# Feed-forward of a streaming encoder step on one core: split weight operands kept in DRAM by the first block and loaded by the others, with the first steps and block borders reordered

## Chip, cores and metric

The kernel runs on one core of one Trainium2 chip. The metric is the device time of one execution in microseconds. Three runs of the kernel before gave 2531.25, 2531.59 and 2532.89 us; their median is 2531.59 us.

## The reference, cut to what matters

All arrays are fp32: 2048 prompt positions and 64 sample positions, model width 1024, one layer. The change lies in the second half of the layer, the convolutional feed-forward, which takes some 1540 of the 2529 us:

```python
def causal_dwconv(u, prev, w):            # width 3, along positions
    up = jnp.concatenate([prev.astype(u.dtype), u], axis=1)
    y = up[:, 0:L] * w[0]
    for t in range(1, width):
        y = y + up[:, t:t + L] * w[t]
    return y, up[:, L:]

def conv_ffn(xn, prev, w_up, conv_w, w_down):     # w_up 1024 x 5632, w_down 2816 x 1024
    u = xn @ w_up
    uc, new = causal_dwconv(u, prev, conv_w)
    a, g = jnp.split(uc, 2, axis=-1)
    return (jax.nn.silu(g) * a) @ w_down, new

    x = x + mixer(rmsnorm(x, norm1))              # first half: gated short convolution and GLA heads
    x = x + conv_ffn(rmsnorm(x, norm2))
return rmsnorm(x, final_norm)
```

## The kernel before

**Blocks.** The positions go through the kernel in three blocks, NB = 3: 768, 768 and 512 + 64 (with a gap of 2 columns between prompt and sample). First all three blocks go through the mixer, then all three through the feed-forward. A block has 6, 6 and 5 tiles of 128 rows (the last of block 2 has 64, and TensorE works on it in another way).

**fp32 from fp32r.** Every product is made of three matmuls on fp32r operands: each operand is split into a high part (ACT's Copy to fp32r) and a low part (operand minus high part, in fp32r), and high x high, low x high and high x low are added (`product`, L1282 to L1284, the lines of the three matmuls).

**Steps.** A feed-forward block has NF = 22 steps; step f makes 128 columns of a and 128 of g from x, and adds their share of the output. `ffn_step` is written once for each engine (SP, POOL, ACT, PE, DVE), and the engines run through the same steps in their own order with semaphores between them. g in the code counts steps over the blocks, g = b * NF + f. Steps 2 to 19 are a hardware loop; steps 0, 1, 20, 21 are written out.

**Seven products.** The up projection of a step is a 2 x 2 block matrix product (columns a and g by two halves of the block's positions, `HALF` = 384, 384, 290, and two halves of the 1024 input features) that is done with seven products instead of eight (a Strassen-Winograd scheme). Its weight operands are three raw quarters (`A_RAW`) and four sums of quarters (`A_SUM`); its x operands are likewise three pieces and four sums, which were written to the DRAM tensor `x_ops` in the mixer stage (`combine` makes the sums S1 to S4 on DVE). Operand i of the weights belongs to product i. A product is 4 x 3 matmuls over 128x128 weights. Its results go to PSUM and are put together with the helpers r_1 (ACT), r_2 and r_3 (DVE); product 2 waits for r_1, 3 for r_2, 5 for r_3, because of the banks.

**Weights of a step.** SP loads the four quarters with two DMAs (`load_up`, L539, to `wu_raw`, one buffer), two steps ahead. DVE makes four sums (`sum_up`, L1639 to L1645, to `wu_sum`). ACT makes seven high parts (`high_up`, L899), POOL seven low parts in two instructions each (`low_up`, L795). The results, `wq_hi` and `wq_lo`, have one buffer per operand: operand i of the next step can be made once product i of this step is done. This is done in every step of every block, 66 times, with the same 22 weight tiles in each block. The w_down tile (128 x 1024) comes by one DMA and is split by ACT (L1237) and POOL (L820).

**Down products.** 12 (block 2: 10) per step, one for each tile and half of 512 columns; each is 3 matmuls (the 64-row tile 2). They are spread over the following two steps by `head_shares` and `tail_shares` (how many after each of the seven products), and use four PSUM banks, which come free when DVE has added the result to `resid` (`add_down`, L1880). `finish_up` on ACT and DVE is the chain from u to the hidden values: taps (L1897), silu (L937), the product with a (L1906); `high_hidden` and `low_hidden` split the hidden values.

**Block borders.** In the last step of a block SP loads the next block's seven x operands (`load_x_op`, L543), each after the product that used its place; in this and the next step ACT splits them (`high_x`) and DVE or POOL makes the low part (`low_x`: DVE 0, 1, 3, 5 in L1630, POOL 2, 4, 6 in L803). In steps 0 and 1 of a block the last block's output is normalised (`final_rstd` on ACT, with a change of the activation table; `final_scale` on DVE, L1608), stored, and the residual tiles of the new block are loaded (`load_resid`); DVE waits for them (`resid_ready`).

**The order.** No scheduler: every engine's order is the order of the text. SP issues all DMAs, on one queue, and where a DMA has to wait for a semaphore, all behind it wait. The lines that say when a step's weights are loaded and when a step's sums are made:

```python
sp.wait_ge(wu_summed, 4 * (g + 2))          # SP, at the end of its step
sp.wait_ge(wu_lo, NP * (g + 1) + 6)
load_up(b, f + 2 ...)
sum_up(g + 1, 0); sum_up(g + 1, 1)          # DVE, between r_2 and r_3
```

## Time and profile before

| | busy us | share of the span | instructions |
|---|---|---|---|
| TensorE matmul (PE) | 2359.5 | 93% | 13090 |
| TensorE weight load (PEld) | 2141.1 | 85% | 13090 |
| VectorE (DVE) | 1802.6 | 71% | 2588 |
| GpSimd (POOL) | 1516.2 | 60% | 1489 |
| ScalarE (ACT) | 1073.9 | 42% | 2059 |

The profiled execution took 2530.73 us, with a span of 2529.0 us from the first to the last recorded instruction. Its mean granted TensorE clock was 0.978 of full. It moved 231 MB, 92 GB/s on average.

The page's slices show the stages (each digit is the busy share of 1/40 of the span, 63 us, in tenths; the feed-forward begins in the 16th):

```profile
PE   7999999999999995999999988999999978888896
DVE  2045670355624566889888897888888879999998
POOL 3132423222343237887788795888888877777773
PEclk9999999999999998999999998999999989999998
```

A busy share counts matmuls with their modelled ends, so a PE that is busy throughout has no gap, but says nothing of how fast one matmul is. Shares are averages over stages with different limits.

### The profile page before, as it was taken

To read this page: it belongs to the slowest core of one execution; us is meant where nothing else is said; L and a number is where in the kernel's file an instruction comes from. 1 tells how busy PE (TensorE), PEld (TensorE's weight loads), DVE (VectorE), ACT (ScalarE), POOL (GpSimd) and SP (SyncE) were. 2 spreads that over 40 slices of the span, in tenths; PEclk is the share of its full clock that TensorE was granted. 3 is DMA by queue.
4 is the path that set the end of the run, shared out by engine and by line. 5 is a ranking of instruction groups with operands and counts; after the bars stand their busy time and mean duration, and the time that the engine had idled before them with its cause. 6 is when DMAs were issued, how large, how long until landed. Compare 5 with 4: busy or idle time off the path is not lost. (4 is left out here: it accounts for less than half of the span.)

```text
span 2529.0 us, 39169 instructions
## 1 busy us (share of the span) xinstructions
PE 2359.5 (93%) x13090; PEld 2141.1 (85%) x13090; DVE 1802.6 (71%) x2588; ACT 1073.9 (42%) x2059; POOL 1516.2 (60%) x1489
## 2 busy tenths in 40 slices
PE   7999999999999995999999988999999978888896
PEld 6899878898798974999999977999999967787785
DVE  2045670355624566889888897888888879999998
ACT  4233353333543335444444455444444464444443
POOL 3132423222343237887788795888888877777773
PEclk9999999999999998999999998999999989999998
DMA  5121334112361146222221244222122432222221
GB/s 158 51 59 43 125 136 143 43 43 101 115 193 51 60 142 230 68 67 75 75 67 57 75 137 150 75 75 75 50 75 75 141 120 74 74 77 75 77 74 65
DMA packets 244718, 231.43 MB, mean 92 GB/s; under 512 B 8060, under 2 KB 216273, under 8 KB 244625
## 3 DMA queue, kind: packets, MB, share of 16 engines
q1 hardware_dynamic: 244625, 230.18, 28.9%
q8 instruction: 60, 0.98, 0.2%
q14 instruction: 33, 0.27, 0.0%
HBM read 197.32 MB, written 32.83 MB: 91 GB/s over the span
## 5 line engine op out<-in xcount | busy, mean ns | idle before, releaser
L1282 PE MATMUL ps<-xo,wq_hi 128*128 128x384 f32 (+1 forms) x1848 | 607.4, 329 | 92.7 <-DVE r L1960 42.3
L795 POOL TENSOR_TENSOR wq_lo<-wu_sum,wq_hi 128x256 fp32r<-128x256 f32 x528 | 478.4, 929 | 213.4 <-ACT wq_hi L899 207.4
L1283 PE MATMUL ps<-xo,wq_lo 128*128 128x384 f32 (+1 forms) x1848 | 603.7, 327 | 0.0
L1284 PE MATMUL ps<-xo,wq_hi 128*128 128x384 f32 (+1 forms) x1848 | 603.3, 326 | 0.0
L458 POOL TENSOR_TENSOR w_lo<-raw,w_hi 128x512 fp32r<-128x512 f32 x192 | 251.0, 1333 | 576.6 <-ACT w_hi L451 576.6
L1880 DVE TENSOR_TENSOR resid<-resid,ps 128x512 f32<-128x512 f32 (+1 forms) x748 | 487.1, 678 | 17.7 <-PE ps L1284 6.2
L1282 PEld LDWEIGHTS ps<-xo,wq_hi 128*128 128x128 f32 x1848 | 355.4, 192 | 127.7 <-issue 73.3
L795 POOL TENSOR_TENSOR wq_lo<-wu_raw,wq_hi 128x256 fp32r<-128x256 f32 x396 | 406.0, 1045 | 35.6 <-ACT wq_hi L899 35.5
L1283 PEld LDWEIGHTS ps<-xo,wq_lo 128*128 128x128 f32 x1848 | 355.7, 192 | 19.1
L1897 DVE SCALAR_TENSOR_TENSOR up_y<-up_u,params,up_y 128x768 f32<-128x768 f32 (+1 forms) x264 | 321.9, 1219 | 49.7 <-ACT up_y L929 26.0
L1284 PEld LDWEIGHTS ps<-xo,wq_hi 128*128 128x128 f32 x1848 | 356.0, 193 | 0.0
L1282 PE MATMUL ps<-xt_hi,w_hi 128*128 128x384 f32 (+4 forms) x960 | 317.0, 330 | 6.8 <-DVE xt_lo L1622 3.8
L1283 PE MATMUL ps<-xt_hi,w_lo 128*128 128x384 f32 (+4 forms) x960 | 310.5, 323 | 0.0
L1284 PE MATMUL ps<-xt_lo,w_hi 128*128 128x384 f32 (+4 forms) x960 | 310.3, 323 | 0.0
L899 ACT ACTIVATE wq_hi<-wu_sum 128x512 fp32r<-128x512 f32 x264 | 163.4, 627 | 318.2 <-DVE wu_sum L1641 204.3
L1282 PE MATMUL ps<-wd_hi,hid_hi 128*128 128x512 f32 x704 | 279.8, 397 | 14.5 <-DVE resid L1880 13.9
L1284 PE MATMUL ps<-wd_lo,hid_hi 128*128 128x512 f32 x704 | 279.9, 398 | 0.0
L1283 PE MATMUL ps<-wd_hi,hid_lo 128*128 128x512 f32 x704 | 277.8, 395 | 0.0
L1282 PEld LDWEIGHTS ps<-xt_hi,w_hi 128*128 128x128 f32 x960 | 182.4, 190 | 19.0 <-issue 8.9
L1283 PEld LDWEIGHTS ps<-xt_hi,w_lo 128*128 128x128 f32 x960 | 182.6, 190 | 5.4 <-issue 0.5
L1284 PEld LDWEIGHTS ps<-xt_lo,w_hi 128*128 128x128 f32 x960 | 182.3, 190 | 5.1
L820 POOL TENSOR_TENSOR wd_lo<-wd_raw,wd_hi 128x512 fp32r<-128x512 f32 x132 | 181.9, 1398 | 2.7 <-ACT wd_hi L1237 2.7
(197 smaller groups left out, 3818.2 us busy)
## 6 DMA issues: line engine op xcount, KB each, us to landing
wu_raw<-in_w_up_dram SPq DMA_DIRECT2D x132, 512.0 KB, 5.0
raw<-in_w_in_dram SPq DMA_DIRECT2D x72, 512.0 KB, 3.8
wd_raw<-in_w_down_dram SPq DMA_DIRECT2D x66, 512.0 KB, 5.7
x_in<-in_x_prompt_dram SPq DMA_DIRECT2D x32, 512.0 KB, 4.4
raw<-in_w_out_dram SPq DMA_DIRECT2D x24, 512.0 KB, 3.3
xo_raw<-x_ops SPq DMA_DIRECT2D x14, 768.0 KB, 5.7
x_mid<-resid SPq DMA_DIRECT2D x16, 512.0 KB, 2.8
resid<-x_mid SPq DMA_DIRECT2D x16, 512.0 KB, 6.2
```

The costliest lines, as they stand in the source:

```text
L458: last = pool.tensor_tensor(w_lo[:, s, r], raw[:, s, r], w_hi[:, s, r].bitcast(F32), ALU.subtract)
L795: last = pool.tensor_tensor(wq_lo[:, i, r], src[:, r], wq_hi[:, i, r].bitcast(F32), ALU.subtract)
L820: last = pool.tensor_tensor(wd_lo[:, par, r], wd_raw[:, r], wd_hi[:, par, r].bitcast(F32), ALU.subtract)
L899: act.activation(wq_hi[:, i, :], wu_source(i), ACT.Copy).then_inc(wu_hi, 1)
L1282: pe.matmul(out, lh, rh, start=(first and n == 0), stop=False, skip_group_check=skip)
L1283: pe.matmul(out, ll, rh, start=False, stop=False, skip_group_check=skip)
L1284: last = pe.matmul(out, lh, rl, start=False, stop=end, skip_group_check=skip)
L1880: last = dve.tensor_tensor(resid[0:m, t, s], resid[0:m, t, s], ps[0:m, bank, :], ALU.add)
L1897: dve.scalar_tensor_tensor(y, up_u[:, m, tap:tap + w], params[:, FFN_TAP + tap, bass.ds(m * NF + f, 1)], y, ALU.mult, ALU.add).then_inc(su ...
```

## The change

- `wq_hi` and `wq_lo` become one tensor `wq` [128, 7, 2, 512], in which the high and low part of an operand lie side by side (`WQ_AT` is the place of operand i).
- A new DRAM tensor `w_ops` holds, for each of the 22 steps, the seven finished operands (high and low, 128 x 4 KB, 0.52 MB each). `KEPT` says which are kept (all seven), `SPLIT` which are still made in each block (all in block 0, none in blocks 1 and 2).
- Block 0: after the low part of operand i SP stores it (`store_op`). ACT's `high_up` waits until the store of the same operand of the step before has read it (`op_stored`).
- Blocks 1 and 2: `high_up` and `low_up` return at once and `sum_up` isn't called. SP loads operand i of the next step in place once product i of this step is done (`load_op`); PE waits for `op_loaded`.
- First step of all: the split of operand 1 moves up; r_1 is copied by ACT before the other x operands (`keep_first_product`); x operands 4, 5 and 6 are split inside step 0; the second half of the last `combine` moves behind r_2; `load_up(0, 1)` and the loads of x operands 5 and 6 move ahead of the stores of the sums, the first w_down tile behind them. The stores of step 0's operands 0 to 5 stand behind that.
- Block borders: `low_x(6)` moves from POOL to DVE. Of the final norms in step 1, tiles 4 and 5 move up on ACT and DVE, with one activation table change fewer, and SP issues their stores and residual loads between the operand loads (`results`).
- Last step of all: no down products of the step before in it; all 10 come behind it.

The diff, cut to its core (declarations, renamed arguments, blank and most unchanged lines are left out):

```diff
@@ -77,6 +77,11 @@
 S1, S2, S3, S4 = 0, 1, 2, 3
 A_RAW = {0: 0, 2: 1, 5: 3}
 A_SUM = {1: S2, 3: S3, 4: S1, 6: S4}
+WQ_AT = [0, 1, 4, 5, 2, 3, 6]
+KEPT = (0, 1, 2, 3, 4, 5, 6)
+SPLIT = [tuple(range(NP))] + 2 * [tuple(i for i in range(NP) if i not in KEPT)]
 X_SUM = {4: 0, 1: 1, 3: 2, 5: 3}
...
@@ -136,11 +141,15 @@
...
+    if b == NB - 1 and isinstance(f, int) and f == NF - 2:
+        return shares([0] * NP, 0)
...
+    if b == NB - 1 and isinstance(f, int) and f == NF - 2:
+        return shares([2 * TILES[b]], 0)
...
@@ -490,6 +503,15 @@
...
+        def after(b, f):
+            return (b + 1, 0) if is_last(f) else (b, f + 1)
+        def splits(b, f, i):
+            steps = NP * f if b == 0 else NP * NF + len(SPLIT[b]) * ((b - 1) * NF + f)
+            return steps + sum(n <= i for n in SPLIT[b])
...
@@ -536,12 +558,36 @@
...
+            def kept(f, i):
+                return w_ops[bass.ds(f, 1), 1 + KEPT.index(i)].rearrange("o p s c -> p (o s) c")
+            def store_op(f, i):
+                sp.wait_ge(wu_lo, splits(0, f, i))
+                sp.dma_start(kept(f, i), wq[:, WQ_AT[i]].bitcast(F32)).then_inc(op_stored[KEPT.index(i)], 16)
+            def load_op(b, f, i):
+                sp.wait_ge(up_done, NP * (b * NF + f - 1) + i + 1)
+                sp.wait_ge(op_stored[KEPT.index(i)], 16 * NF)
+                sp.dma_start(wq[:, WQ_AT[i]].bitcast(F32), kept(f, i)).then_inc(op_loaded[KEPT.index(i)], 16)
...
@@ -653,50 +699,79 @@
...
+                if b == NB - 1:
+                    sp.wait_ge(wu_lo, splits(0, 0, 5))
+                    load_up(0, 1)
                 sp.wait_ge(x_sums, sums_before(b + 1))
+                if b == NB - 1:
+                    sp.wait_ge(ops_stored, 16 * 3 * NB)
+                    for i in range(5, NP):
+                        load_x_op(0, i)
                 for i, n in X_SUM.items():
...
+                if b == NB - 1:
+                    second[b].wait(sp, "turned", 2 * nt)
+                    sp.wait_ge(sums_stored, 16 * 4 * NB)
+                    load_down(0)
...
+                if b == 0 and edge == 0:
+                    for i in KEPT:
+                        if i < 6:
+                            store_op(f, i)
                     for t in range(TILES[0]):
                         load_resid(0, t)
-                wait(sp, wd_low, g)
-                sp.dma_start(wd_raw[:, :], w_down[0, bass.ds(f * P, P), :]).then_inc(wd_loaded, 16)
...
+                else:
+                    wait(sp, wd_low, g)
+                    load_down(f)
+                if b == 0:
+                    store_op(f, 6)
+                nb, nf = after(b, f)
+                then = after(nb, nf)
+                for i in range(NP):
+                    if edge == NF - 1 and b + 1 < NB:
                         sp.wait_ge(up_done, NP * g + i + 1)
                         load_x_op(b + 1, i)
...
+                    if more and i in KEPT:
+                        if nb:
+                            load_op(nb, nf, i)
+                        elif i < 6:
+                            store_op(nf, i)
...
+                    if edge == 1 and b and i in (1, 3):
+                        results(b, range(i + 1, min(i + 3, TILES[b - 1])))
+                if load and not nb and SPLIT[then[0]]:
+                    sp.wait_ge(wu_lo, splits(nb, nf, 5))
+                    load_up(*then)
+                if edge == 0 and b:
+                    results(b, range(2))
...
@@ -788,11 +863,13 @@
...
-            def low_up(g, i):
-                pool.wait_ge(wu_hi, NP * g + i + 1)
+            def low_up(b, f, i):
+                if i not in SPLIT[b]:
+                    return
+                pool.wait_ge(wu_hi, splits(b, f, i))
                 src = wu_source(i)
                 for r in (slice(0, 256), slice(256, 512)):
-                    last = pool.tensor_tensor(wq_lo[:, i, r], src[:, r], wq_hi[:, i, r].bitcast(F32), ALU.subtract)
+                    last = pool.tensor_tensor(wq[:, WQ_AT[i], 1, r], src[:, r], wq[:, WQ_AT[i], 0, r].bitcast(F32), ALU.subtract)
                 last.then_inc(wu_lo, 1)
...
@@ -823,33 +900,26 @@
...
+            low_up(0, 0, 0)
+            low_up(0, 0, 1)
             low_x(0, 2)
...
-            low_x(0, 6)
+            for i in range(2, NP - 1):
+                low_up(0, 0, i)
...
                 if first_f:
                     low_x(b, 4)
                 for i in range(NP - 1):
                     if more:
-                        low_up(g + 1, i)
-                    if i == 4:
+                        low_up(*after(b, f), i)
+                    if i == (5 if first_f and b == 0 else 4):
                         low_down(g, par)
-                        if first_f:
-                            low_x(b, 6)
                 if is_last(f) and b + 1 < NB:
                     low_x(b + 1, 2)
...
@@ -895,8 +965,27 @@
...
-            def high_up(g, i):
-                act.activation(wq_hi[:, i, :], wu_source(i), ACT.Copy).then_inc(wu_hi, 1)
+            def high_up(b, f, i):
+                if i not in SPLIT[b]:
+                    return
+                g = b * NF + f
+                if i in A_RAW:
+                    act.wait_ge(wu_loaded[A_RAW[i] // 2], 16 * (g + 1))
+                    if b == 0 and i == 5:
+                        act.wait_ge(wu_summed, 4 * g + 4)
+                else:
+                    act.wait_ge(wu_summed, 4 * g + A_SUM[i] + 1)
+                if b == 0 and i in KEPT:
+                    wait(act, op_stored[KEPT.index(i)], 16 * g)
+                act.activation(wq[:, WQ_AT[i], 0], wu_source(i), ACT.Copy).then_inc(wu_hi, 1)
+            def keep_first_product(b, g, par):
+                h = HALF[b]
+                act.wait_ge(up_done, NP * g + 1)
+                wait(act, c21_read, g)
+                act.activation(r_1[:, 0:h], ps[:, 3 * par, 0:h], ACT.Copy).then_inc(r1_read, 1)
...
@@ -1168,75 +1264,69 @@
...
+                            high_up(0, 0, 0)
+                            high_up(0, 0, 1)
                         if j == 2:
                             high_x(0, 1)
...
-                            high_up(0, 1)
-                        if j == 4:
                             high_x(0, 2)
-                        if j == 5:
-                            high_up(0, 2)
+                        if j == nt:
+                            mix.wait(act, "out_done", 8 * nt)
+                            high_up(0, 0, 2)
+                            keep_first_product(0, 0, 0)
...
+            high_up(0, 0, 3)
+            high_x(0, 3)
+            high_up(0, 0, 4)
+            high_up(0, 0, 5)
...
-                high_up(g, 6)
+                if not first_of_all:
+                    keep_first_product(b, g, par)
+                high_up(b, f, 6)
                 if prev:
                     high_hidden(*prev, 1 - par)
-                if edge == 0 and b:
+                if edge == 0:
                     high_x(b, 4)
...
-                    act.preload_act_table(ACT.Silu)
...
+                    act.wait_ge(up_done, NP * g + 1)
+                    high_up(nb, nf, 0)
                     act.wait_ge(up_done, NP * g + 2)
-                    act.wait_ge(wu_summed, 4 * (g + 1) + S2 + 1)
-                    high_up(g + 1, 1)
+                    high_up(nb, nf, 1)
                 act.wait_ge(up_done, NP * g + 3)
                 wait(act, taps_a, 2 * g)
                 act.activation(up_u[:, 0, 2:2 + h], ps[:, 3 * par, 0:h], ACT.Copy).then_inc(c11_read, 1)
                 earlier_rows(b, 0, f)
-                if edge == 0 and b:
+                if edge == 0:
                     high_x(b, 5)
                 if more:
-                    high_up(g + 1, 2)
+                    high_up(nb, nf, 2)
                     act.wait_ge(up_done, NP * g + 4)
-                    act.wait_ge(wu_summed, 4 * (g + 1) + S3 + 1)
-                    high_up(g + 1, 3)
+                    high_up(nb, nf, 3)
                     act.wait_ge(up_done, NP * g + 5)
-                    high_up(g + 1, 4)
...
+                    high_up(nb, nf, 4)
+                if not first_of_all:
+                    high_down(b, f, par)
+                if edge == 0:
                     high_x(b, 6)
+                if edge == 1 and b:
+                    for t in range(4, TILES[b - 1]):
+                        final_rstd(b - 1, t)
+                    act.preload_act_table(ACT.Silu)
...
@@ -1247,13 +1337,15 @@
...
+                    high_up(nb, nf, 5)
+                if first_of_all:
+                    high_down(b, f, par)
...
-                if edge in (0, 1) and b:
+                if edge == 0 and b:
                     act.preload_act_table_set("natural_log_exp_and_others")
-                    for t in range(2) if edge == 0 else range(4, TILES[b - 1]):
+                    for t in range(2):
                         final_rstd(b - 1, t)
...
@@ -1542,7 +1634,10 @@
...
-                    pe.wait_ge(wu_lo, NP * g + i + 1)
+                    if i in SPLIT[b]:
+                        pe.wait_ge(wu_lo, splits(b, f, i))
+                    else:
+                        pe.wait_ge(op_loaded[KEPT.index(i)], 16 * (g - NF + 1))
...
@@ -1858,15 +1955,17 @@
...
-                    if b == NB - 1:
-                        for c0, w in PIECES[b].get(j - 2, []):
-                            n2.wait(dve, "hi", 2 * (j - 2))
-                            done = combine(c0, w)
+                    if b == NB - 1 and j == nt:
+                        n2.wait(dve, "scaled", nt)
+                        sum_up(0, 1)
+                        n2.wait(dve, "hi", 2 * 3)
+                        done = combine(b, *PIECES[b][3][0], done)
...
@@ -1921,9 +2020,11 @@
...
-            sum_up(0, 1)
             low_x(0, 3)
-            low_x(0, 5)
+            def last_combine():
+                second[NB - 1].wait(dve, "hi", 2 * TILES[NB - 1])
+                combine(NB - 1, *PIECES[NB - 1][5][0], sums_before(NB - 1) + 4)
...
@@ -1948,18 +2049,20 @@
...
                 dve.tensor_tensor(r_2[:, 0:h], ps[:, 1, 0:h], r_1[:, 0:h], ALU.add).then_inc(r2_read, 1)
+                if edge == 0 and b == 0:
+                    last_combine()
...
                 adds(1)
-                if more:
+                if b == 0 and not is_last(f):
                     sum_up(g + 1, 0)
                     sum_up(g + 1, 1)
                 adds(2)
                 dve.wait_ge(up_done, NP * g + 4)
                 dve.tensor_tensor(r_3[:, 0:h], ps[:, 1, 0:h], r_1[:, 0:h], ALU.add).then_inc(r3_read, 1)
...
-                if edge == 0 and b:
+                if edge == 0:
                     low_x(b, 5)
...
@@ -1967,6 +2070,11 @@
...
                 adds(4)
+                if edge == 0:
+                    low_x(b, 6)
+                if edge == 1 and b:
+                    for t in range(4, TILES[b - 1]):
+                        final_scale(b - 1, t)
...
```

## Rows read from the trace of the kernel before

**Rows 1.** The windows view, core 0: stretch, busy us, instructions, clock, DMA share, GB/s.

```profile
1080.00:1440.00 360.00, 360.00 (x1895) 336.76 (x1894) 322.10 (x412) 152.15 (x254) 286.63 (x286) 1.00 0.22 67
1600.00:1980.00 380.00, 380.00 (x2000) 355.45 (x2000) 330.74 (x435) 164.01 (x302) 311.39 (x298) 1.00 0.23 70
2077.81:2480.22 402.41, 358.27 (x2129) 321.52 (x2128) 368.26 (x534) 180.09 (x446) 310.92 (x361) 0.97 0.26 78
2480.22:2497.32 17.10, 16.77 (x108) 15.38 (x106) 15.63 (x25) 5.89 (x17) 9.26 (x10) 1.00 0.09 32
...
957.62:1025.29 67.67, 38.14 (x200) 35.47 (x200) 44.71 (x43) 30.54 (x48) 56.15 (x54) 0.82 0.60 206
1481.56:1580.94 99.38, 78.29 (x362) 71.19 (x361) 78.18 (x90) 52.72 (x90) 73.24 (x68) 0.88 0.36 119
2014.39:2077.81 63.42, 45.49 (x239) 40.22 (x237) 50.49 (x63) 36.76 (x70) 48.68 (x50) 0.87 0.38 126
...
970.00:994.00 24.00, 6.30 (x23) 6.33 (x24) 8.89 (x10) 8.91 (x10) 17.32 (x20) 0.53 1.00 347
1464.00:1470.00 6.00, 6.00 (x33) 5.51 (x32) 5.97 (x9) 2.78 (x5) 5.44 (x6) 1.00 0.98 374
```

**Rows 2.** The timeline of PE, block 2: first matmul of a product, down product, product.

```profile
2166.36 0.29 PE L1282 MATMUL ps<-xo,wq_hi 128*128 128x290 f32 x1
...
2167.97 0.39 PE L1282 MATMUL ps<-wd_hi,hid_hi 128*128 128x512 f32 x1
...
2169.34 0.29 PE L1282 MATMUL ps<-xo,wq_hi 128*128 128x290 f32 x1
```

**Rows 3.** Groups by line and form, DVE, 2100 to 2480: busy us, mean ns.

```profile
L1897 DVE SCALAR_TENSOR_TENSOR up_y<-up_u,params,up_y 128x578 f32<-128x578 f32 x73 | 92.3, 1264 | 18.6 <-ACT up_y L929 13.3 <-DVE up_y L1897 3.8
...
L1639 DVE TENSOR_TENSOR wu_sum<-wu_raw 128x512 f32<-128x512 f32 x18 | 20.4, 1133 | 0.0
L1641 DVE TENSOR_TENSOR wu_sum<-wu_sum,wu_raw 128x512 f32<-128x512 f32 x18 | 20.0, 1113 | 0.6
...
L1643 DVE TENSOR_TENSOR wu_sum<-wu_raw 128x512 f32<-128x512 f32 x18 | 13.3, 740 | 0.0
```

**Rows 4.** Who waited for whom, 2100 to 2480: us in total, times, longest.

```profile
PE ps L1282 <- DVE r L1960: 28.5, 16, 1.9
```

**Rows 5.** Groups by form, DVE, 2500 to 2503, where POOL does nothing.

```profile
L1897 DVE SCALAR_TENSOR_TENSOR up_y<-up_u,params,up_y 128x578 f32<-128x578 f32 x2 | 1.6, 822 | 0.1
```

**Rows 6.** The timeline of PE at start and border 0/1; in brackets the idle time before.

```profile
987.70 0.66 PE L1282 MATMUL ps<-xo,wq_hi 128*128 128x384 f32 x1 [21.35 <-ACT r L1203]
...
996.74 0.41 PE L1282 MATMUL ps<-xo,wq_hi 128*128 128x384 f32 x1 [0.27 <-DVE r L1960]
...
1518.09 0.66 PE L1282 MATMUL ps<-xo,wq_hi 128*128 128x384 f32 x1 [5.43 <-issue]
...
1542.09 0.56 PE L1282 MATMUL ps<-xo,wq_hi 128*128 128x384 f32 x1 [4.79 <-DVE r L1960]
...
1564.85 0.79 PE L1282 MATMUL ps<-wd_hi,hid_hi 128*128 128x512 f32 x1 [5.01 <-DVE resid L1880]
```

**Rows 7.** The timeline of SP, POOL and DVE, single lines.

```profile
972.33 3.75 SPq L658 DMA_DIRECT2D x_ops<-tst  x4
...
1512.69 5.29 POOL L803 TENSOR_TENSOR xo<-xo_raw,xo 128x384 fp32r<-128x384 f32 x4
...
1703.42 0.80 DVE L1639 TENSOR_TENSOR wu_sum<-wu_raw 128x512 f32<-128x512 f32 x1
...
1718.37 1.00 SPq L539 DMA_DIRECT2D wu_raw<-in_w_up_dram  x2
```

**Rows 8.** The page's DMA issues: KB each, median us from issue to landing.

```profile
wu_raw<-in_w_up_dram SPq DMA_DIRECT2D x132, 512.0 KB, 5.0
...
x_mid<-resid SPq DMA_DIRECT2D x16, 512.0 KB, 2.8
```

120 lines of the change are left out of this document (49 added, 71 removed).

## The prediction, made before the changed kernel ran

> **What bounds the kernel now.** The windows view comes first, cut at the borders that PE's timeline shows. In the middle of block 0's feed-forward PE is busy 360.00 of 360 us at granted clock 1.00 [rows 1]; 1895 matmuls make 0.190 us each, so a step of 120 matmuls (7 products of 12, 12 down products of 3) takes 22.8 us. Block 1's middle is the same (2000 matmuls in 380.00 us). Nothing that ACT, DVE, POOL or SP is spared there shortens the step. In block 2 (steps 2 to 20) PE is busy 358 of 402 us at clock 0.97, and DVE 368 [rows 1]: 21.18 us a step. Its floor: a product of 12 matmuls of 290 columns takes 2167.97 - 2166.36 = 1.61 us, six down matmuls 2169.34 - 2167.97 = 1.37 us [rows 2], so 84 x 0.134 + 28 x 0.228 = 17.7 us. The waits view names who holds PE: product 5, behind DVE's r_3 (L1960), 1.8 us in 16 of 18 steps [rows 4]; after it the clock is at the lower of its two levels for some matmuls, which is how 1.8 us become 3.5. DVE is late because of the four sums of sum_up, which stand just ahead of r_3: 20.4 + 20.0 + twice 13.3 (L1643; L1645 has the same) = 67.0 us over 18 steps, 3.7 us a step [rows 3]. The last step of all is the experiment in the old kernel: no sums, POOL nearly empty, 17.10 us with PE busy 16.77 [rows 1].
>
> The other losses are the borders, three stretches that [rows 1] hold as well: start of block 0 (957.62 to 1025.29, PE busy 38.1 of 67.7), border 0/1 (1481.56 to 1580.94, 78.3 of 99.4), border 1/2 (2014.39 to 2077.81, 45.5 of 63.4). All three also run at clock 0.82 to 0.88.
>
> **Part 1: no split in blocks 1 and 2.** Gone: 44 x 7 high parts on ACT, 44 x 14 low halves on POOL, 44 x 4 sums on DVE. Block 1's middle: 0 us, since PE is full. Block 2: DVE is busy 368.26 / 19 = 19.4 us a step, less 3.7 is 15.7 us, at the pace it has beside POOL, plus 18.6 / 18 = 1.0 us of waits before the taps [rows 3]: 16.7 against PE's 17.7. PE takes over. But the margin of 1.0 us is thin, and in the last step, with POOL still busy in its first part, PE still lost 0.3 us. So how fast DVE is without POOL matters. The taps (128x578) take 1264 ns in the middle of block 2 [rows 3] and 822 ns where POOL does nothing [rows 5]; four a step give 1.8 us more margin. I take 17.9 us a step (floor plus 0.2), bounds 17.7 (floor) and 19.4 (only the 1.8 us of idle go, and smaller waits keep pulling the clock down). 19 steps: 402.4 - 340.1 = **-62 us** (-67 to -34).
>
> The Trainium skill ("SBUF — State Buffer", section "Who interferes with whom") has the rule behind those taps: a VectorE instruction with two SBUF inputs and a GpSimd instruction that reads SBUF need the same read interface, and the one that comes second waits. 822 against 1264 ns is as the rule says. By it all the contended time goes away and the step sits at 17.7 to 17.9; without it DVE would keep 16.7 us of work, and I would take 18.4, a sum 10 us worse.
>
> **Part 2: what replaces it, transfers.** A step now loads 7 x 0.524 MB of operands and 0.524 MB of w_down: 4.19 MB, in block 2 in 17.9 us, 234 GB/s, where 78 is moved now [rows 1]. The trace has stretches with the queues full: 347 GB/s over 24 us, with stores among them, 374 over 6 us [rows 1]. PE is 6.00 of 6 us busy in the latter with 33 matmuls, 0.18 each, so full queues do not slow it. Each operand is asked for when PE has finished that product of the step before and is wanted a whole step less one product later, some 16 us, for a landing of 5.0 us [rows 8]. Hidden; cost 0, and if the rate fell under 234 GB/s it would show at once. SP's load of w_down now stands behind the load of operand 6, which waits for the step's last product; ACT wants it four products later, at least 10 us, and a load of this size lands in 5. Hidden.
>
> **Part 3: block 0 pays.** Seven stores of 0.524 MB a step: 5.24 MB in 22.8 us, 230 GB/s. The new wait, ACT's high part of operand i on the store of the previous step's, has a whole step of slack in the middle. The load of step f+2's weights now has one more store in front of it, 1.4 us at 374 GB/s: issued at 1718.37 and landed 5.0 us later at 1723.4 now, at about 1725 then; its first DVE reader comes at 1703.42 + 22.8 = 1726.2 [rows 7, 8]. Hidden by 1 us, and DVE has more slack after it. Cost 0, bounds 0 and +0.6 x 20 = +12 us.
>
> **Part 4: border 0/1.** Three steps of 120 matmuls at 0.190 are 68.4 us; 99.4 is taken. The stalls: product 6 of step 0 waits 5.43 us for low_x(6), which POOL ends at 1512.69 + 5.29 [rows 6, 7]; it stands behind seven low parts that go, and moves to DVE, which no longer has its sums. Product 5 of step 1 waits 4.79 us for r_3, behind two final scales and the four sums. In step 2 a down product waits 5.01 us for DVE, which stands at the wait for the residual tiles 4 and 5 [rows 6]; their final scales and stores move up by some 5 us. I let 8 us stay (the taps chain of step 0, final scales): **-23** (-12 to -29). What is late next is the wait for gated and low_x(3), 2 to 3 us.
>
> **Part 5: border 1/2.** Floor: 168 x 0.134 + 69 x 0.228 = 38.2 us; 63.4 is taken. DVE is busy 50.5 us there, less two steps of sums 43.1. So DVE, not PE, is the next bound: I take 45, **-18** (-8 to -23).
>
> **Part 6: start of block 0.** Now PE idles 21.35 us before product 2, since ACT copies r_1 only after all x operands [rows 6]. The copy moves up behind high_up(2), to about 964. Walking the new order by hand at today's durations (low_x on POOL 5.3 us [rows 7]), product 2 can start at 967, product 3 at 971, product 4 at 979 (POOL's low_x(4)). But look at what product 5 waits for. ACT's order in step 0 is high_x(4), high_up of step 1's operands 0 and 1, copy c11, high_x(5). Those high_up wait for the stores of step 0's operands 0 and 1. SP issues these stores only behind load_down(0), and that stands behind the landing of the four sums (2.4 MB), which are issued at 972.33 now [rows 7], and in the new order after the last combine, which moves behind low_x(3) and r_2 (about 977), and behind x operands 5 and 6 (128 x 1536 fp32 each, 1.6 MB): 4 MB at 347 to 374 GB/s and about 2 us to land is 989, then 0.5 + 0.5 MB and landing (2.8 us for such a store [rows 8]): 993. All of ACT stands till then: the c11 copy, high_x(5), high_x(6). Product 5 starts about 998.5 (996.74 now [rows 6]), product 6 about 1002. So the 21 us that were idle before product 2 are idle before product 5. Then step 1: between 989 and the landing of step 2's weights SP moves 11.5 MB (w_down, 13 stores, 6 residual tiles, the weights): 31 us at 370, so about 1019 instead of 1012, and DVE's sums hold r_3 again. **+6 us** (-10 if the stores get through early, +14).
>
> **Part 7: the end.** Four down products move from the last step behind it. DVE is back to back there and has the same additions: 0 (±1).
>
> Sum: -62 - 23 - 18 + 6 = -97. The profiled execution took 2530.7 (span 2529.0 and 1.7 around it): 2433.4; the median lies 0.9 above it: **2434 us**.
>
> **Rivals.** (A) DVE keeps block 2: the chain finish_up, adds, r_2, r_3 is serial, and 19.4 us a step remain, with less at the borders (-17, -12): -34 - 29 + 6 = -57, 2475 us. For it: DVE is still busy 15.7 of 17.7. Against it: the last step. (B) The start gives time back: if SP's stores get through 10 us earlier than reckoned, or ACT's wait is met, product 5 starts near 985 and the start is 12 us shorter, not 6 longer: 2416. For it: everything but that one wait is ready. Against it: SP issues in order. (C) The other side: the transfers become the bound. The feed-forward moves 22 x 5.24 + 44 x 4.19 = 300 MB, with the borders some 325, in the 1540 us from 957 to 2497; at under 211 GB/s sustained it is longer than before. At 200 it is 325 / 0.200 - 1540 = 85 us longer, 2616. For it: no stretch in the trace keeps up such a rate for more than some 30 us. Against it: 347 over 24 us with writes among it. (D) Block 0's stores don't hide: 1.5 us a step over 20 steps, for example by the weights' landing past DVE's need: 2464.
>
> **Chances.** Forecast 0.62 (own range 2420 to 2450), A 0.12, B 0.12, C 0.04, D 0.10. Range 2412 to 2474: it takes in B and D, and ends at A; outside lie C and the far ends of A. About 0.2% (5 us) can be told from no change: faster 0.95, same 0.01, slower 0.04.
>
> **What would show it.** Block 2's steps at 17.7 to 18.1 us and clock 1.00, taps near 0.82 us there (A if 19.4); blocks 0 and 1 unchanged at 22.8 us a step (D if block 0 is longer); DMA near 230 GB/s through the feed-forward; the wait of product 6 at the borders gone; at the start ACT idle for some 15 us ahead of a wq high part, released by SP's store, and PE's long idle before product 5. The prediction is wrong if any step of blocks 1 or 2 waits for an operand's load, or if the start is shorter than before.

## The result, and the profile after

The changed kernel takes **2447.14 us** (median of 4 runs, 2444.29 to 2447.52), the kernel before 2532.24 us beside it: ratio 0.9662, 95% interval 0.9649 to 0.9675, 85.1 us less. The forecast was 2434 us in a range of 2412 to 2474. The profiled span went from 2529.0 to 2445.4 us. Cut at the first matmul of an up product (product 0 of the step named), the two traces and a third one (the reordering alone, experiment 1) give this table; the last two columns are differences, changed minus before:

| stretch, us | before | reordering alone | changed | forecast | measured |
|---|---|---|---|---|---|
| up to the first up product | 957.6 | 957.5 | 956.6 | 0 | -1.0 |
| start of block 0 (to step 2) | 67.7 | 62.5 | 82.3 | +6 | **+14.6** |
| rest of block 0 | 456.3 | 456.3 | 456.3 | 0 | 0 |
| border 0/1 (to step 3) | 99.4 | 88.5 | 80.9 | -23 | **-18.5** |
| rest of block 1 | 433.5 | 433.5 | 433.5 | 0 | 0 |
| border 1/2 (to step 2) | 63.4 | 58.0 | 46.4 | -18 | **-17.0** |
| block 2, steps 2 to 20 | 402.4 | 401.0 | 338.8 | -62 | **-63.6** |
| last step and end | 48.8 | 50.4 | 50.7 | 0 | **+2.0** |

The windows view of the changed kernel, columns as in [rows 1], which hold the matching stretches of before. In order: the middle of block 0, the middle of block 1, block 2 (steps 2 to 20), the start, border 0/1, border 1/2:

```profile
1080.00:1440.00 360.00, 360.00 (x1894) 336.64 (x1893) 322.53 (x411) 152.64 (x254) 284.80 (x282) 1.00 0.65 229
1600.00:1950.00 350.00, 350.00 (x1844) 327.46 (x1842) 236.72 (x339) 92.55 (x168) 69.95 (x62) 1.00 0.58 185
2055.89:2394.67 338.78, 336.99 (x2130) 314.12 (x2129) 271.35 (x465) 109.14 (x309) 80.58 (x95) 1.00 0.76 243
956.61:1038.87 82.26, 43.98 (x200) 40.50 (x200) 44.23 (x45) 30.25 (x48) 55.35 (x50) 0.75 0.81 290
1495.13:1575.99 80.86, 72.25 (x361) 64.84 (x360) 63.38 (x79) 38.76 (x67) 23.62 (x20) 0.98 0.73 268
2009.45:2055.89 46.44, 40.41 (x239) 36.77 (x237) 36.81 (x53) 27.78 (x57) 16.81 (x16) 0.96 0.76 267
```

In block 2 PE is busy 336.99 of 338.78 us at clock 1.00, where it was 358 of 402 at 0.97; DVE has 14.3 us of work a step (271.35 / 19) instead of 19.4. In the start the clock is at 0.75 and PE idle for 38 of 82 us, while the queues move 290 GB/s. By form, DVE's taps in block 2 (2100 to 2380, as [rows 3]):

```profile
L1996 DVE SCALAR_TENSOR_TENSOR up_y<-up_u,params,up_y 128x578 f32<-128x578 f32 x64 | 52.6, 822 | 14.9 <-ACT up_y L1018 10.2 <-DVE up_y L1996 3.3
```

The wait of product 5 for r_3 [rows 4] is gone from block 2: the longest wait of its steps 2 to 20 is 0.9 us, once, for an addition. The page's DMA issues (as [rows 8]):

```profile
wq<-w_ops SPq DMA_DIRECT2D x308, 512.0 KB, 3.8
w_ops<-wq SPq DMA_DIRECT2D x154, 512.0 KB, 2.7
```

The start in the timelines of ACT, SP, PE and DVE, in that order (the number in brackets is the idle time before, and who ended it):

```profile
968.59 1.47 ACT L994 ACTIVATE xo<-xo_raw 128x1536 fp32r<-128x1536 f32 x1
998.17 0.63 ACT L982 ACTIVATE wq<-wu_raw 128x512 fp32r<-128x512 f32 x1 [28.12 <-DMA w_ops<-wq]
...
978.41 6.35 SPq L712 DMA_DIRECT2D x_ops<-tst  x4
992.65 0.34 SPq L590 DMA_DIRECT2D wd_raw<-in_w_down_dram  x1
993.10 6.16 SPq L576 DMA_DIRECT2D w_ops<-wq  x6
...
1012.97 6.41 SPq L561 DMA_DIRECT2D wu_raw<-in_w_up_dram  x2
...
1003.69 0.66 PE L1374 MATMUL ps<-xo,wq 128*128 128x384 f32 x1 [17.97 <-issue]
...
1029.10 0.66 PE L1374 MATMUL ps<-xo,wq 128*128 128x384 f32 x1 [4.71 <-DVE r L2063]
...
1025.60 0.95 DVE L1736 TENSOR_TENSOR wu_sum<-wu_raw 128x512 f32<-128x512 f32 x1 [6.45 <-issue]
```

ACT stands 28.12 us before its first high part of step 1, until step 0's operand 0 is stored. The stores were issued at 993.10, behind w_down, which waited for the landing of the four sums. PE waits 17.97 us before product 5 (the view says "issue" because it sees no releaser; ACT's high part of x operand 5 ends at 1001.8 and DVE's low part at 1003.6). That is the forecast mechanism; but it is 5 us later, and a second one stands behind it: step 2's weights land at about 1025 (forecast 1019), and r_3 comes only behind DVE's sums of them.

### The profile page after: what moved, and what is told of

It reads as the page before. It is cut to its first block and busy times, and to the rows that moved or that the text cites. A ratio compares the mean times of both kernels' runs of the same rounds, so it can differ in the third digit from the quotient of the medians.

```text
span 2445.4 us, 39112 instructions
## 1 busy us (share of the span) xinstructions
PE 2332.6 (95%) x13090; PEld 2129.1 (87%) x13090; DVE 1583.6 (65%) x2415; ACT 906.9 (37%) x1747; POOL 919.7 (38%) x861
## 5 line engine op out<-in xcount | busy, mean ns | idle before, releaser
L1374 PE MATMUL ps<-xo,wq 128*128 128x384 f32 (+1 forms) x1848 | 600.0, 325 | 46.4 <-issue 18.6
L1375 PE MATMUL ps<-xo,wq 128*128 128x384 f32 (+1 forms) x1848 | 598.8, 324 | 0.0
L1376 PE MATMUL ps<-xo,wq 128*128 128x384 f32 (+1 forms) x1848 | 598.6, 324 | 0.0
L1374 PEld LDWEIGHTS ps<-xo,wq 128*128 128x128 f32 x1848 | 350.8, 190 | 68.2 <-issue 46.7
L1375 PEld LDWEIGHTS ps<-xo,wq 128*128 128x128 f32 x1848 | 351.3, 190 | 20.4
L1376 PEld LDWEIGHTS ps<-xo,wq 128*128 128x128 f32 x1848 | 351.3, 190 | 0.0
L1996 DVE SCALAR_TENSOR_TENSOR up_y<-up_u,params,up_y 128x768 f32<-128x768 f32 (+1 forms) x264 | 272.7, 1033 | 49.1 <-ACT up_y L1018 30.7
L897 POOL TENSOR_TENSOR wd_lo<-wd_raw,wd_hi 128x512 fp32r<-128x512 f32 x132 | 170.2, 1310 | 313.5 <-ACT wd_hi L1049 313.5
L1374 PE MATMUL ps<-wd_hi,hid_hi 128*128 128x512 f32 x704 | 277.5, 394 | 10.8 <-DVE resid L1979 10.4
L891 POOL TENSOR_TENSOR hid_lo<-up_y,hid_hi 128x384 fp32r<-128x384 f32 (+1 forms) x132 | 120.1, 931 | 254.4 <-ACT hid_hi L1042 254.4
L872 POOL TENSOR_TENSOR wq<-wu_sum,wq 128x256 fp32r<-128x256 f32 x176 | 161.9, 945 | 62.8 <-ACT wq L982 60.3
L1374 PE MATMUL ps<-w_hi,xt_hi 128*128 128x512 f32 (+1 forms) x408 | 163.7, 401 | 6.3 <-issue 2.9
```

The lines of the kernel that those rows point to most:

```text
L872: last = pool.tensor_tensor(wq[:, WQ_AT[i], 1, r], src[:, r], wq[:, WQ_AT[i], 0, r].bitcast(F32), ALU.subtract)
L891: last = pool.tensor_tensor(hid_lo[:, par, r], up_y[:, 0, r], hid_hi[:, par, r].bitcast(F32), ALU.subtract)
L897: last = pool.tensor_tensor(wd_lo[:, par, r], wd_raw[:, r], wd_hi[:, par, r].bitcast(F32), ALU.subtract)
L1374: pe.matmul(out, lh, rh, start=(first and n == 0), stop=False, skip_group_check=skip)
L1375: pe.matmul(out, ll, rh, start=False, stop=False, skip_group_check=skip)
L1376: last = pe.matmul(out, lh, rl, start=False, stop=end, skip_group_check=skip)
```

## Experiments

Times are medians; "the changed kernel" is 2447.1 us. Stretches are cut as in the table. Seven profiles with the changed kernel's start unaltered have 80.1 to 82.7 us there; among the kernels that leave the borders as they are, border 0/1 has 77.9 to 81.4 and border 1/2 45.1 to 47.8. So a single one of these stretches is known to some 2 us.

**1. The reordering without the keeping.**

```
-KEPT = (0, 1, 2, 3, 4, 5, 6)
+KEPT = ()
-                if b == 0 and not is_last(f):
+                if more:
                     sum_up(g + 1, 0)
```
(and the weights of every step loaded whole by `load_up`)

> The reorderings of the change without the keeping: every step of all three blocks loads and splits its weights as before the change (KEPT is empty, DVE's sums and POOL's low parts are back in blocks 1 and 2, no operand is stored or loaded). Theory (block 2's gain is the splitting's, the start's loss is the kept stores'): block 2's steps 2 to 20 stay near 402 us, start of block 0 near 60 to 66 us instead of 82.3 (67.7 before the change), since ACT is held by no store; border 0/1 some 8 us under the 99.4 of before, border 1/2 some 4 under its 63.4; in all 2532 - 4 - 8 - 4 = 2516 us (2505 to 2525). Rival 1 (the borders' gain is all the reordering's): 2532 - 4 - 18.5 - 17 = 2492. Rival 2 (the start's loss is the reordering's, not the stores'): the start stays near 80, and the time is 2532 + 12 - 12 = 2532.

Measured 2510.75 us, ratio to before 0.9919 (0.9902 to 0.9935), before at 2531.1 in this set: some 20 us of the 85 are the reordering's, some 65 the keeping's. The table's middle column splits them by place: the start gains 5.2 us by the reordering and loses 19.8 by the keeping; border 0/1 gains 10.8 and 7.7, border 1/2 5.4 and 11.6; block 2 1.4 and 62.2. Most of what the end lost (1.6 us) is the reordering's. Both rivals are out. Block 2 is as before the change, waits included (the second line is of the waits view: total, times, longest):

```profile
2056.28:2457.24 400.96, 355.60 (x2129) 318.77 (x2128) 367.26 (x533) 175.20 (x439) 310.83 (x363) 0.98 0.25 76
...
PE ps L1368 <- DVE r L2057: 34.2, 19, 1.9
```

**2 to 4. Which engine's work held block 2.** Idle work, whose result nothing reads, is put back into blocks 1 and 2 of the changed kernel (the waits around it are left out):

```
 low_up (POOL):  if i not in SPLIT[b]:
+    for r in (slice(0, 256), slice(256, 512)):
+        last = pool.tensor_tensor(wu_raw[:, 1 + 2 * (i % 2), r], wu_raw[:, 0, r], wu_raw[:, 2, r], ALU.subtract)
 ffn_step (DVE), where sum_up stood:
+if b:
+    for n in range(4):
+        dve.tensor_tensor(wu_sum[:, n, :], wu_raw[:, 0, :], wu_raw[:, 2, :], ALU.add)
```

> The changed kernel with POOL's work of blocks 1 and 2 put back as idle work: 14 subtractions of 128x256 a step on scratch that nothing reads, at the places of the low parts; no sums on DVE, no high parts on ACT, operands loaded as in the change. By the trace before the change DVE's 128x578 taps take 1264 ns beside POOL and 822 without it. Theory (the Trainium skill, "SBUF — State Buffer", section "Who interferes with whom": VectorE with two SBUF inputs waits for GpSimd's SBUF reads): the taps take 1.1 to 1.3 us again, DVE is busy some 16.4 us a step instead of 14.2, still under PE's 17.7, so block 2 runs at 17.9 to 18.5 us a step, 2449 to 2460 us in all. Rival 1 (it was the contention that made block 2 late): 19.5 or more a step, over 2478 us. Rival 2 (the taps were slow for another reason, the sums or the weights' loads): taps stay at 0.82 us.

> The changed kernel with DVE's four sums a step put back in blocks 1 and 2 as idle work on scratch (four additions of 128x512 just ahead of the second group of additions and r_3, as they stood before); POOL stays nearly idle. Each should take 0.69 us as in block 0 when POOL is quiet, 2.8 us a step. Theory (DVE's serial work just ahead of r_3 is what held product 5, but it takes POOL's contention too to reach PE's pace): DVE busy 17.0 us a step, block 2 at 18.0 to 18.8 us a step, 2451 to 2466 us. Rival (the sums alone made block 2 late): 20 or more a step, over 2487 us. Block 1 unchanged by either.

> Both idle works together, POOL's 14 subtractions and DVE's four additions a step in blocks 1 and 2, everything else as in the change. Theory (the two together are what block 2 paid; ACT's high parts cost nothing there): 21.0 us a step in block 2, 60 us more than the changed kernel, near 2507 us, taps at 1.25 us, the sums at 1.1 us for the first two. Rival (DVE and POOL account for less, ACT's high parts or the weights' place in the queue for the rest): 18.5 to 20 us a step.

| | total | block 2, per step | borders 0/1, 1/2 |
|---|---|---|---|
| changed | 2447.1 | 17.83 | 80.9, 46.4 |
| POOL's work | 2461.4 | 18.43 | 82.5, 48.8 |
| DVE's sums | 2459.7 | 17.69 | 86.2, 54.4 |
| both | 2522.8 | 20.87 | 87.4, 57.8 |

DVE by form in block 2: the taps and an addition out of PSUM beside POOL's work; the sums without and with it:

```profile
L2004 DVE SCALAR_TENSOR_TENSOR up_y<-up_u,params,up_y 128x578 f32<-128x578 f32 x64 | 74.5, 1164 | 15.4 <-ACT up_y L1026 10.6 <-DVE up_y L2004 3.5
L1987 DVE TENSOR_TENSOR resid<-resid,ps 128x512 f32<-128x512 f32 x124 | 80.5, 679 | 3.5 <-PE ps L1384 3.5
```

```profile
L2063 DVE TENSOR_TENSOR wu_sum<-wu_raw 128x512 f32<-128x512 f32 x76 | 47.4, 688 | 0.0
```

```profile
L2071 DVE TENSOR_TENSOR wu_sum<-wu_raw 128x512 f32<-128x512 f32 x76 | 88.2, 1218 | 0.0
```

The sums alone cost block 2 nothing, POOL alone 0.6 us a step, the two together 3.0, almost all that block 2 had lost (3.35). Neither was "the" cause. Each lengthens DVE's step: its work is 14.3 us a step in the changed kernel, 15.9 beside POOL's work, 16.2 with the sums, and 19.2 with both, where each sum takes 1218 instead of 688 ns. Only that is past PE's 17.7 us, and only there product 5 waits for r_3 again, in all 19 steps:

```profile
PE ps L1382 <- DVE r L2074: 46.7, 19, 3.0
```

ACT's high parts were put back in none of the three; what stays open is the last 0.3 us a step, in which they may have a part. The Trainium skill ("SBUF — State Buffer", section "Who interferes with whom") has it that a VectorE instruction with two inputs in SBUF contends with a GpSimd instruction that reads SBUF; the rows agree: taps 822 to 1164 ns, sums 688 to 1218, the addition with one input in PSUM unchanged at 679 (681 in the changed kernel). I had reckoned POOL's work alone at 17.9 to 18.5 (18.43), the sums alone at 18.0 to 18.8 (17.69: too dear), both at 21.0 (20.87). What the sums do cost is the borders, 5.4 and 7.9 us, where PE waits for DVE. I had left the borders out. So the total with the sums alone, 2459.7, lies in the range expected (2451 to 2466) by luck, and the total with both, 2522.8, is 16 us above the 2507 expected: block 2 has 57.7 us of the 75.6, the borders 6.5 and 11.4.

**5. The transfers' ceiling.** Behind each kept operand's load one more of 0.524 MB into scratch (two behind operand 6), eight a step:

```
                             load_op(nb, nf, i)
+                            more_loads(nb, nf, i)
```

> The changed kernel with eight more loads of 0.524 MB a step in blocks 1 and 2, of operands just stored, into scratch that nothing reads: 8.4 MB a step instead of 4.2, 470 GB/s if block 2 kept 17.8 us a step. Theory (the transfers have a ceiling at the 370 to 420 GB/s that full queues show at the start of block 0, and the change stands well below it): the steps of block 2 become as long as the bytes take, 8.4 / 0.400 = 21 us (20 to 23), block 1's 22.8 us stay or grow to at most 23 since they ask for 368 GB/s. Total 2500 to 2560 us. Rival (the sustained ceiling is lower than such short stretches show, 250 to 300 GB/s): 28 to 33 us a step in both blocks, over 2650 us.

Measured 2517.1 us. The windows of blocks 2 and 1:

```profile
2069.00:2457.00 388.00, 354.82 (x2126) 311.69 (x2124) 282.70 (x461) 106.52 (x305) 83.03 (x93) 1.00 1.02 408
1600.00:1950.00 350.00, 350.00 (x1841) 327.32 (x1841) 237.36 (x340) 94.27 (x171) 69.25 (x62) 1.00 0.99 369
```

Block 2 took 20.48 us a step: 408 GB/s held over 388 us with the DMA engines busy throughout (share 1.02), and the step as long as its bytes (16 x 0.524 MB). PE itself waits only 3.0 us for operands; most of the delay comes by w_down's tile, which lands late behind the other loads, and ACT stands for it in each of the 19 steps:

```profile
ACT wd_hi L1060 <- DMA wd_raw<-in_w_down_dram: 172.4, 19, 9.9
```

Block 1 at 369 GB/s lost nothing, PE 350.00 of 350 us. So the change, at 243 and 185 GB/s, stands well under the ceiling in every middle stretch; rival C is out for the middle of the blocks.

**6 to 10. The start.** First SP's order alone (6): the stores of step 0's operands ahead of the sums' stores and of w_down.

```
                     load_up(0, 1)
+                    for i in range(2): store_op(0, i)
 ...                 load_x_op(0, 5); load_x_op(0, 6)
+                    for i in range(2, 6): store_op(0, i)
 ...                 (and no longer in ffn_step)
```

> The stores of step 0's kept operands are moved on SP: those of operands 0 and 1 right behind the load of step 1's weights, those of 2 to 5 behind the loads of x operands 5 and 6, all ahead of the stores of the four x sums and of the load of w_down. Theory (ACT stands 28.12 us at the wait for operand 0's store, and all of ACT with it): operand 0's store lands near 985 instead of 998, ACT's high_x(5) runs near 989, product 5 of step 0 starts near 992 instead of 1003.7, everything behind it slides by as much; the stretch from the first up product to that of step 2 goes from 82.3 us to 66 to 72, and the time from 2447 to 2431 to 2437. Rival (the x operands' landing or the sums' stores hold product 5, not the kept operands' stores): the stretch stays within 4 us of 82, the time at 2443 to 2447. Everywhere else no change.

Measured 2447.7 us: no gain. Yet ACT and product 5 did as expected. ACT, PE, SP and DVE:

```profile
984.01 0.63 ACT L983 ACTIVATE wq<-wu_raw 128x512 fp32r<-128x512 f32 x1 [13.07 <-DMA w_ops<-wq]
...
990.48 0.66 PE L1375 MATMUL ps<-xo,wq 128*128 128x384 f32 x1 [4.32 <-issue]
...
1008.71 11.37 SPq L561 DMA_DIRECT2D wu_raw<-in_w_up_dram  x2
...
1027.21 0.96 DVE L1737 TENSOR_TENSOR wu_sum<-wu_raw 128x512 f32<-128x512 f32 x1 [15.27 <-DMA wu_raw<-in_w_up_dram]
```

Product 5 starts 13.2 us earlier, and step 2's weights land no earlier: DVE stands 15.27 us for them, and all 13 us are given back. The early stores also push other work back: the last of the sums lands at 1001.2 instead of 992.6, and w_down, which SP issues only behind that landing, goes out at 1001.21 instead of 992.65. Next (7), the 3 MB of residual tiles moved behind those weights:

```
                     load_up(*then)
+                if b == 0 and edge == 0:
+                    for t in range(TILES[0]): load_resid(0, t)
```

> As the kernel before in this set (stores of step 0's operands early), and the six residual tiles of block 0 (3 MB) are loaded behind the load of step 2's weights instead of ahead of step 1's stores. Theory (the queues are full between 996 and 1020, and step 2's weights land some 11 us behind their issue, because 3 MB of residual tiles and seven stores stand before them; DVE's sums then hold r_3 of step 1): the weights of step 2 land within 4 us of their issue, the 4.7 us that product 5 of step 1 waits for r_3 go, and the start is 4 to 8 us shorter than with the early stores alone, about 2427 us in all. Rival (the issue is late, not the landing: it waits for POOL's low part of operand 5 of step 1): no more than 1 us against the early stores alone.

Measured 2440.0 us, 7.1 under the changed kernel: the start took 71.7 instead of 82.3, the rest of block 0 458.3 instead of 456.3, since now the residual tiles are late. The step from the kernel before it, 7.7 us, is in the range expected, and the rival is out (the start alone became 11.3 us shorter, of which the rest of block 0 gave 2 back); the total expected, 2427, had counted in the first kernel's gain, which did not come. Nothing fewer was moved: what DVE waits for was put ahead of what is needed later. Two more reorderings (8 and 9) took further waits away: ACT's high part of x operand 6 moved up (with the last step's shares of experiment 11), then in step 1 DVE's sums behind r_3 and ACT's copy of c11 up.

```
 ACT, step 0:  high_x(b, 5)
+              if first_of_all: high_x(b, 6)
```

> Three edits on the changed kernel together: step 0's stores early with the residual tiles behind step 2's weights (2440.0 us so measured), the last step's shares as before the change (2.5 to 3 us shorter so measured), and on ACT in block 0's first step the high part of x operand 6 right behind that of operand 5, no longer behind the three wq high parts that wait for the kept stores. Theory (what is left of the start's loss is ACT at those waits, 6.6 us between products 5 and 6 against 3.7 with no stores at all): product 6 of step 0 starts some 2.5 us earlier; the start is then bound by the transfers (355 GB/s and more from 976 to 1036), so at most 1 us of it reaches product 0 of step 2. Sum 2440.0 - 2.8 - 1 = 2436 us (2434 to 2438). Rival (products, not transfers, bound step 1): the 2.5 us arrive whole, 2434.

```
 DVE, step 1:  dve.tensor_tensor(r_3[:, 0:h], ps[:, 1, 0:h], r_1[:, 0:h], ALU.add).then_inc(r3_read, 1)
+              if b == 0 and edge == 1: sum_up(g + 1, 0); sum_up(g + 1, 1)     # no longer ahead of r_3
 ACT, step 1:  act.activation(up_u[:, 0, 2:2 + h], ps[:, 3 * par, 0:h], ACT.Copy).then_inc(c11_read, 1)
+              if early: high_up(nb, nf, 0); high_up(nb, nf, 1)                # no longer ahead of the copy
```

> As the kernel before in this set, and in step 1 of block 0 DVE makes the sums of step 2's weights behind r_3 instead of ahead of it, and ACT copies product c11 ahead of its two high parts of step 2, so that neither product 5 nor the taps of step 1 wait for the landing of step 2's weights. Theory (the landing of those weights is what the start ends on): product 5 of step 1 loses its 2.7 us of idle, but product 1 of step 2 needs the sums a few us later, so 1 to 3 us shorter than without these two, 2433 to 2435 us. Rival (the wait only moves to step 2's products): no difference, 2436.

Measured 2437.65 us and **2436.19 us** (2434.86 to 2438.14, ratio 0.9626, 0.9610 to 0.9642). The first brought product 6 forward by 2.7 us (993.48) and nothing at product 0 of step 2: product 2 of step 1 waited 7.7 us instead of 3.0 for ACT. What it gained on the kernel before it, 2.4 us, is the end's. The second took 1.1 us off start and block 0 together, which is within the scatter, and a wait of 2.96 us came up in step 2 for additions. Each of these waits came back behind another landing, and both times it is w_down's: ACT stands for it in step 1 of the first kernel (and in step 2 of the second, 5.40 us). Below are that row, then SP's issue of w_down in the second kernel and its windows around that issue:

```profile
1004.49 1.06 ACT L1048 ACTIVATE wd_hi<-wd_raw 128x1024 fp32r<-128x1024 f32 x1 [8.71 <-DMA wd_raw<-in_w_down_dram]
...
1000.31 0.34 SPq L586 DMA_DIRECT2D wd_raw<-in_w_down_dram  x1
...
1000.20:1002.20 2.00, 1.03 (x6) 0.71 (x5) 0.00 (x0) 0.00 (x0) 0.00 (x0) 1.00 0.47 111
1002.20:1006.00 3.80, 0.00 (x0) 0.00 (x0) 0.00 (x0) 1.79 (x3) 0.65 (x1) 0.99 0.99 365
```

SP still issues w_down, and all that stands behind it, only when the four sums have landed, and meanwhile the queue runs empty: 111 GB/s, then 365. No run loads w_down ahead of the sums' stores. What was tested is the stores (10): the last kernel without the seven of step 0. Since it leaves them out, blocks 1 and 2 take step 1's operands in their step 0 and compute something else; only its time counts.

```
-                    for i in range(2): store_op(0, i)
-                    for i in range(2, 6): store_op(0, i)
-                if b == 0:
+                if b == 0 and edge != 0:
                     store_op(f, 6)
-                    wait(act, op_stored[KEPT.index(i)], 16 * g)
+                    wait(act, op_stored[KEPT.index(i)], 16 * (g - 1))
 ...                 (load_op waits for 16 * (NF - 1) and takes step 1's operands for step 0)
```

> The last kernel of the set before (2436.2 us: early stores, residual tiles late, x operand 6 early, step 1's sums behind r_3, last step's shares as before the change) without the seven stores of block 0's step 0 and without ACT's waits for them in step 1; blocks 1 and 2 take step 1's operands in their step 0, so this part of the result is another one. 3.67 MB less are moved between 976 and 1005, 10 us at the 355 GB/s of that stretch. Theory (the start of block 0 and the few steps behind it are bound by the transfers: from 976 to 1036 they run at 347, 322 and 369 GB/s, and every wait that was taken away came back as another wait for a landing): the stretch from the first up product to that of block 1, 529.6 us in that kernel and 518.8 with the reordering alone, becomes 7 to 11 us shorter, 519 to 522, and the time 2426 to 2429 us. Rival (what is left is the order of the engines' own work, not the bytes): 0 to 3 us shorter, 2433 to 2436.

Measured 2427.4 us, 8.8 less. Start and rest of block 0 together: 538.5 us in the changed kernel, 539.2 with the early stores, 530.0, 530.7 and 529.6 with the following three, 521.4 without step 0's stores, 518.8 with the reordering alone. The windows from 976 to 1036 of the last two kernels, with and without those stores:

```profile
976.00:996.00 20.00, 9.60 (x31) 9.34 (x32) 8.66 (x11) 7.44 (x10) 14.46 (x17) 0.66 0.94 347
996.00:1016.00 20.00, 13.33 (x64) 12.56 (x63) 8.27 (x8) 5.32 (x10) 9.92 (x9) 0.83 0.93 322
1016.00:1036.00 20.00, 16.71 (x80) 14.66 (x79) 12.10 (x16) 8.00 (x14) 13.54 (x16) 0.93 0.95 369
```

```profile
976.00:996.00 20.00, 12.10 (x43) 11.65 (x44) 11.06 (x12) 7.40 (x10) 16.11 (x18) 0.66 0.89 285
996.00:1016.00 20.00, 17.03 (x93) 15.92 (x92) 11.33 (x16) 7.76 (x14) 15.27 (x17) 1.00 1.04 385
1016.00:1036.00 20.00, 17.67 (x84) 15.77 (x83) 15.76 (x19) 8.05 (x15) 12.41 (x12) 0.91 0.86 311
```

The forecast of 7 to 11 us came from the bytes alone (3.67 MB at 355 GB/s), and the rival is out. But two waits went with the bytes. One is ACT's for the stores; experiment 6 had shortened the first of those by 15 us for nothing. The other is SP's for the sums' landing: without stores ahead of it w_down is issued 8.0 us earlier than at the 1000.31 above (7.2 counted from the first up product), about as much as was gained:

```profile
992.28 0.34 SPq L586 DMA_DIRECT2D wd_raw<-in_w_down_dram  x1
```

So it is shown that step 0's stores, with the waits that hang on them, cost 8.8 us in that kernel; whether as bytes, or because SP waits behind them, is not.

**11. The last step's shares as before the change.**

```
 head_shares, tail_shares:
-    if b == NB - 1 and isinstance(f, int) and f == NF - 2:
-        return shares([0] * NP, 0)        # tail_shares: shares([2 * TILES[b]], 0)
```

> The shares of down products and additions in the last step of all as they were before the change (head and tail shares of block 2's step 20 spread over step 21, no down products moved behind the last up product). Theory (the moved down products made the end longer, 48.78 to 50.73 us from the first up product of the last step, because PE waits 3.6 us for DVE's additions with nothing else to do): the end is 1 to 3 us shorter, the rest unchanged, 2444 to 2446 us. Rival (the end's length comes from elsewhere, DVE being back to back there): within 0.5 us of the changed kernel, or longer.

Measured 2444.6 us (2442.3 to 2445.8, which overlaps the changed kernel's runs; the stretch tells it): the end took 47.96 us instead of 50.73, its idle of 3.62 us gone, and the two kernels above with the same edit have 48.0 as well. The rest of the difference in that profile is its start, 80.1 us, within the scatter. The row of the changed kernel:

```profile
2416.09 0.50 PE L1374 MATMUL ps<-wd_hi,hid_hi 128*128 128x512 f32 x1 [3.62 <-DVE resid L1979]
```

Behind the last up product PE has nothing but down products: the four moved there wait, with all of the last step's, for additions that DVE makes only after the taps.

**12. The low part of x operand 6 back on POOL in blocks 1 and 2.**

```
-        LOW_BY_V = (0, 1, 3, 5, 6)
+        LOW_BY_V = [(0, 1, 3, 5, 6), (0, 1, 3, 5), (0, 1, 3, 5)]
```

> The changed kernel with the low part of x operand 6 back on POOL in blocks 1 and 2 (on DVE in block 0, as in the change), behind w_down's low parts. POOL is nearly empty there now; DVE has 1.8 us (128x1536) less in the first step of each block. The idle work on DVE made border 0/1 5.4 us and border 1/2 7.9 us longer, for 2.8 us a step in two and a half steps: DVE is the bound at the borders. Theory: each border is 0.5 to 1.8 us shorter, 2444 to 2446 us. Rival (the move to DVE is what took away the 5.4 us that product 6 waited at border 0/1): product 6 waits for POOL again, the borders are 1 us or more longer, 2448 us or more.

Measured 2457.1 us, 10 slower: the rival held, not my theory. PE before product 6, then POOL, at border 0/1:

```profile
1525.79 0.66 PE L1376 MATMUL ps<-xo,wq 128*128 128x384 f32 x1 [4.34 <-issue]
```

```profile
1517.86 2.55 POOL L897 TENSOR_TENSOR wd_lo<-wd_raw,wd_hi 128x512 fp32r<-128x512 f32 x2 [5.65 <-ACT wd_hi L1051]
1520.37 5.33 POOL L880 TENSOR_TENSOR xo<-xo_raw,xo 128x384 fp32r<-128x384 f32 x4
```

Even on an idle POOL the work is late, since it stands behind w_down's low part, which waits for ACT, and takes 5.33 us where DVE takes 1.8. Border 0/1 is 4.7 us longer, border 1/2 3.0. The 1.8 us that DVE was spared did not outweigh that.

## Why the prediction was right or wrong

**Block 2 (-62, measured -63.6): right, and for the reason given.** PE took over at 17.83 us a step (17.9 said), the taps came to 822 ns as in [rows 5], clock 1.00. The rule of the Trainium skill ("SBUF — State Buffer", section "Who interferes with whom") by which I chose 17.9 rather than 18.4 held: experiment 2, with the sums gone and POOL's work kept, has 18.43 a step. Rival A (DVE keeps block 2 at 19.4) fell. One reading of the old kernel was too simple: the 1.8 us of idle for r_3 don't become 3.5 by the clock alone. PE's idle in block 2 was 44.1 us, 2.3 a step, since it waited for other things too; the other 1.2 are longer busy time, of which the mean clock of 0.97 over 402 us explains some 0.6. (The bound of -67 should read -66: 402.4 less 19 x 17.7.)

**Transfers (0) and block 0's stores (0): right.** The middles of blocks 0 and 1 are as long as before to the hundredth of a microsecond (456.27 and 433.45), and no step of blocks 1 and 2 waits for an operand's load; experiment 5 puts the ceiling at 408 GB/s. Rivals C and D fell in the middle of the blocks. Of the signs, "near 230 GB/s through the feed-forward" was loosely put: block 1 moves 4.19 MB in 22.8 us, 184 by the prediction's own terms, 185 measured. In the start the queues were full for a while (367 GB/s from 993 to 1025), which is C's mechanism, locally.

**Border 0/1 (-23, measured -18.5).** The 8 us that I let stay as idle are there within 0.6 (80.86 - 72.25 = 8.6). The term that was too low is the floor: 68.4 us at full speed, where PE was busy 72.25 us for the same matmuls. Some 1.6 of these 3.9 us are the clock, which is at the lower level in a single stretch of the border:

```profile
1495.13:1560.75 65.62, 57.01 (x290) 50.89 (x289) 53.57 (x64) 35.71 (x62) 19.10 (x16) 1.00 0.76 283
1560.75:1564.16 3.41, 3.41 (x10) 2.85 (x10) 3.14 (x6) 0.50 (x3) 1.98 (x2) 0.50 1.03 408
```

The other 2.3 us are the edges of the stalls, at clock 1.00. In a row a matmul of 384 columns starts every 0.17 us, but the last one before a stall counts with its whole 0.34, and the first behind it takes longer (0.51 us here, where the next ones of 512 columns take 0.39 to 0.40):

```profile
1504.27 0.33 PE L1375 MATMUL ps<-xo,wq 128*128 128x384 f32 x1
1504.44 0.34 PE L1376 MATMUL ps<-xo,wq 128*128 128x384 f32 x1
1507.12 0.51 PE L1374 MATMUL ps<-wd_hi,hid_hi 128*128 128x512 f32 x1 [2.34 <-DVE resid L1979]
```

That makes up to 0.3 us for each of the eight or nine stalls, on top of the idle time. The step on low_x(6) was right (product 6 waits 0.68 us instead of 5.43), and experiment 12 adds that it was the move to DVE, not POOL's relief, that took the wait away.

**Border 1/2 (-18, measured -17.0): the number right, in part by luck.** The prediction took 45 us from DVE's total work, 43.1. But DVE had 36.8 us of work there, less than PE's 40.4, since without POOL's contention its instructions are shorter. So it isn't DVE's total that bounds the stretch; it is PE's work and 6.0 us of waits for DVE, which experiment 3's sums made longer.

**Start (+6, measured +14.6; range to +14): the mechanism right, two terms mis-sized.** ACT's wait for op_stored held product 5, as said; it was 28.12 us long, not "some 15": ACT reached it at 970.05, so even a landing at 993 would have made 23. "Landing 993" was about 998: I issued the sums' stores at once and let 4 MB flow at 347 to 374 GB/s from 977, but SP took 6.35 us to issue them and the stretch 976 to 996 moved 279 GB/s. And "step 2's weights about 1019" were 1025: the sums landed at 992.6 instead of 989, and the 11.5 MB behind them took 33 us instead of 31. What the prediction missed is that these bytes and product 5's wait run side by side: the end of the start hangs on the landing, so a shorter wait of product 5 is worth nothing. Rival B (the stores get through early, the start gains 12) named the right place and the wrong worth: experiment 6 got them through 14 us earlier, and gained nothing.

**End (0 ±1, measured +2.0): wrong, outside its bounds.** "DVE is back to back there and has the same additions" overlooked that the moved products' additions now stand behind the taps, so that PE waits 3.62 us for them; experiment 11 took that wait away, and the end was 47.96 us.

Of the 13 us between 2434 and 2447, the start has 8.6, border 0/1 4.5, the end 2.0, border 1/2 1.0; block 2 (1.6) and the time up to the first product (1.0, within its scatter of 956.5 to 958.1) give some back.

## What to carry to other kernels

Replacing arithmetic by transfers is cheap where the queues have room: 243 GB/s cost nothing here, where 408 could be had. Where they are full, find the landing on which the stretch ends, and count the bytes ahead of it. Taking a wait away elsewhere gained nothing (experiment 6); putting 3 MB that were needed later behind that landing gained 7 us (experiment 7). An issue that waits for a landing lets the queue run empty, so look for those as well. When a serial engine has two burdens, test each alone and both together; here nothing and 0.6 us made 3.0. Give a border a floor that holds what each stall adds to PE's busy time at its edges, and the clock behind it, and not only the matmuls at full speed. The best version found keeps the change and orders the start and end anew: 2436.2 us against 2447.1 (2437.7 without the last of the reorderings, which the runs can't tell from it).

## What the runs showed of the hardware that was not expected

- A core moved 408 GB/s over 388 us and 369 GB/s with PE busy 350.00 of 350 us, not slower by a matmul.
- While the queues were full (376 GB/s from 1008 to 1020 in experiment 6), issuing was slow as well: two issues of 512 KB took 11.37 us on SP where they took 1.00 [rows 7].
- In experiment 5 the step's phases shifted and a single tap fell beside POOL's w_down low part: it took 1.89 us, the three others 0.82 each.
- The slowing goes both ways: POOL's idle subtraction of 128x256 took 808 ns on average beside the changed kernel's DVE work (experiment 2) and 921 with DVE's sums back as well (experiment 4).
